# Hierarchical MoE block: top-two by the eight largest, gather and gate product by halves, one w_down load moved ahead of two up matrices

## What is computed

```python
    g_top_p, g_top = lax.top_k(g_prob, 1)
    e_in_group = jnp.take_along_axis(e_logits, g_top[:, :, None], axis=1)[:, 0]
    e_top_logit, e_top = lax.top_k(e_in_group, EXPERT_TOPK)
    gate = g_top_p * jax.nn.softmax(e_top_logit, axis=-1)
    ...
    h = (jax.nn.silu(jnp.einsum('td,edf->tef', xt, w_gate))
         * jnp.einsum('td,edf->tef', xt, w_up)
         * combine[..., None].astype(x.dtype))
    return jnp.einsum('tef,efd->td', h, w_down).reshape(nb_, s_, d_)
```

## Time and profile before

| what | value |
|---|---|
| median of 3 runs | 416.0 us (415.92 to 416.49) |
| the profiled execution | 415.13 us |
| its span, first to last instruction | 413.4 us |
| PE busy / weight loads / DVE / ACT / POOL | 90% / 73% / 40% / 33% / 8% of the span |
| DMA, mean over the span | 321 GB/s |
| mean granted TensorE clock | 0.963 of full speed |

### The profile page before, as it was taken

How to read it: one execution, slowest core, us unless ns; L and a number is a source line. 1 busy time by engine, 2 the same in 40 slices (tenths; PEclk the granted TensorE clock), 3 DMA queues, 4 the chain that set the end, 5 groups by cost and what they waited for, 6 DMA issues and landing times.

```text
span 413.4 us, 8388 instructions
## 1 busy us (share of the span) xinstructions
PE 373.6 (90%) x3461; PEld 302.3 (73%) x3461; DVE 166.4 (40%) x334; ACT 135.6 (33%) x235; POOL 33.3 (8%) x46
## 2 busy tenths in 40 slices
PE   7899899999999999999799999968797398499993
PEld 7899898889899999999767676744565156257653
DVE  2653667777264645554640212191202002012026
ACT  3553455734445444425523131301213013011010
POOL 7000000000000000001000002393000000000004
PEclk9999999999999999999999999998899599599998
DMA  8789884766568676699869999999999999999932
GB/s 275 204 316 371 278 291 153 269 219 205 188 203 298 184 253 186 212 412 426 364 230 423 419 420 422 419 419 418 423 420 420 422 419 421 420 421 419 380 104 101
DMA packets 51956, 132.78 MB, mean 321 GB/s; under 512 B 2978, under 2 KB 37810, under 8 KB 40660
## 3 DMA queue, kind: packets, MB, share of 16 engines
q1 hardware_dynamic: 51620, 132.14, 83.7%
q0 software_dynamic: 304, 0.17, 0.3%
HBM read 131.25 MB, written 1.05 MB: 320 GB/s over the span
## 4 chain that ended last, share of the span: by engine, by line
PE 66%; DMA 13%; DVE 9%; SPq 7%; ACT 3%; issue 2%; POOL 0%; DVEq 0%; ACTq 0%; POOLq 0%
PE bank L1073 25%; DMA gu<-in_w_up 13%; PE bank L1314 11%; PE bank L1192 5%; PE bank L1346 5%; SPq L375 5%; PE bank L1125 4%; PE bank L1269 4%; PE bank L1355 3%; PE bank L1169 3%; DVE wl L752 2%; PE bank L1081 2%; ACT wh L592 1%; SPq L380 1%; PE bank L1237 1%
## 5 line engine op out<-in xcount | busy, mean ns | idle before, releaser
L752 DVE TENSOR_TENSOR wl<-raw,wh 128x1024 fp32r<-128x1024 f32 x54 | 65.9, 1224 | 65.8 <-ACT wh L592 65.5
L1073 PE MATMUL bank<-xh,wh 128*128 128x256 f32 x288 | 82.8, 287 | 1.5 <-DVE wl L798 1.5
L1073 PE MATMUL bank<-xl,wh 128*128 128x256 f32 x288 | 81.5, 283 | 0.0
L1073 PE MATMUL bank<-xh,wl 128*128 128x256 f32 x288 | 81.4, 283 | 0.0
L1314 PE MATMUL bank<-gu,xg 128*32 128x256 f32 x1024 | 63.2, 408 | 19.6 <-DMA gu<-in_w_up 19.6
L592 ACT ACTIVATE wh<-raw 128x1024 fp32r<-128x1024 f32 x54 | 56.7, 1056 | 61.8 <-PE bank L1073 34.4
L1314 PEld LDWEIGHTS bank<-gu,xg 128*32 128x32 f32 x1024 | 34.4, 117 | 46.0 <-issue 27.1
L1073 PEld LDWEIGHTS bank<-xh,wh 128*128 128x128 f32 x288 | 55.2, 192 | 4.1 <-issue 2.0
L1073 PEld LDWEIGHTS bank<-xl,wh 128*128 128x128 f32 x288 | 55.2, 192 | 0.2 <-issue 0.2
L1073 PEld LDWEIGHTS bank<-xh,wl 128*128 128x128 f32 x288 | 55.2, 192 | 0.0
L1269 PE MATMUL bank<-pick,x1p 128*128 128x128 f32 x288 | 33.7, 275 | 1.3 <-DVE pick L957 1.3
(11 more groups left out here) (205 smaller groups left out, 469.6 us busy)
## 6 DMA issues: line engine op xcount, KB each, us to landing
gu<-in_w_up SPq DMA_DIRECT2D x32, 1024.0 KB, 23.4
gu<-in_w_gate SPq DMA_DIRECT2D x28, 1024.0 KB, 18.8
dn<-in_w_down SPq DMA_DIRECT2D x25, 1024.0 KB, 16.2
raw<-in_w_in SPq DMA_DIRECT2D x40, 512.0 KB, 4.7
raw<-in_w_o SPq DMA_DIRECT2D x8, 512.0 KB, 4.6
gu<-in_w_gate SPq DMA_DIRECT2D x8, 512.0 KB, 7.7
raw<-in_w_out_conv SPq DMA_DIRECT2D x4, 512.0 KB, 3.6
raw<-in_w_out_attn SPq DMA_DIRECT2D x4, 512.0 KB, 4.6
```

Source lines behind the costliest of these rows:

```text
L752: dve.tensor_tensor(wl[:, s, :].rearrange("p (k c) -> p k c", k=KC), raw[:, pair % NRAW, :].rearrange("p (k c) -> p k c", k=KC) [:, :, n % ...
L1073: mm = pe.matmul(dst, w[:, k, :], v[:, i, :], start=(i == 0 and w is h and v is high_in), stop=(i == len(ks) - 1 and w is l))
```

## The change

Five edits.
- The two `first_max` on 32 columns and the masking between them are replaced by `dve.max` (the eight largest of a row) and `dve.max_index` (their positions), once per tile each, and one compare of the first two positions with 0 to 31, which makes both hot rows.
- `slot_id` starts at FAR in place of 0, so `rank` keeps its offset and L952 goes. The counts (L951) are taken behind `pick_slots(0)`, waited for, and `rank_read` is signalled by an engine_nop.
- `gather(c, g)` makes half g. Half 0 stands where gather stood (the first needs only `pick_done` and `x1p_done`); half 1 is issued between k = 3 and k = 4 of the gate product. The wait for the picks is one per tile, at the first chunk.
- DVE's first `take_gathered` goes behind the gates' weights and `weigh_slots(1, 0)`.
- SP issues two of quad 2's four w_up matrices behind quad 1's last w_down. WARM_ROUTE goes from 14 to 9.

```diff
-WARM_ROUTE = 14
+WARM_ROUTE = 9
...
             sp.wait_ge(gu_ps, over)
-            load_gu(0, 2, parts=[1])
+            load_gu(0, 2, [0, 1], parts=[1])
             sp.wait_ge(y_ps, NY * over)
             for e in range(NE_EARLY, QE):
                 load_dn_one(1, e)
+            load_gu(0, 2, [2, 3], parts=[1])
             for e in range(NE_EARLY):
                 load_dn_one(2, e)
...
-            first_max(masked, expert_key[:, :], NE, top1, eq, hot1, tmp)
-            link(dve.scalar_tensor_tensor(masked, hot1, 100.0 * MASKED, masked, ALU.mult, ALU.add))
-            first_max(masked, expert_key[:, :], NE, top2, eq, hot2, tmp)
+            for t in range(TT):
+                ins = dve.max(top[:, t, :], masked[:, t, :])
+            link(ins)
+            for t in range(TT):
+                ins = dve.max_index(top_id[:, t, :], top[:, t, :], masked[:, t, :])
+            link(ins)
+            link(dve.tensor_tensor(hot[:, :, :, :], expert_id[:, :].unsqueeze(1).unsqueeze(1).to_broadcast(
+                [P, TT, 2, NE]), top_id[:, :, 0:2].unsqueeze(3).to_broadcast([P, TT, 2, NE]), ALU.is_equal))
...
-            dve.tensor_reduce(rf[:, 0, NQ:2 * NQ], counts, AX.X, ALU.max).then_inc(rank_read, 1)
-            link(dve.tensor_scalar(rank[:, :, :], rank[:, :, :], -FAR, None, ALU.add))
...
             pick_slots(0)
+            link(dve.tensor_reduce(rf[:, 0, NQ:2 * NQ], counts, AX.X, ALU.max))
+            dve.engine_nop().then_inc(rank_read, 1)
...
-            take_gathered(1)
...
             weigh_slots(1, 0)
+            take_gathered(1)
...
-            def gather(c):
-
-                pe.wait_ge(pick_done, 2 * c + 2)
-                for k in range(KC):
+            def gather(c, g):
+
+                for k in range(g * KHALF, (g + 1) * KHALF):
                     for t in range(TT):
-                        mm = pe.matmul(bank[4 + k // 4][:, (k % 4) * P:(k % 4 + 1) * P], x1p[:, t, k, :],
+                        if g == 0 and k == 0:
+                            pe.wait_ge(pick_done, 2 * c + t + 1)
+                        mm = pe.matmul(bank[4 + g][:, (k % 4) * P:(k % 4 + 1) * P], x1p[:, t, k, :],
                                        pick[:, t, :, :].rearrange("p e s -> p (e s)"),
                                        start=(t == 0), stop=(t == TT - 1))
-                    if k % 4 == 3:
-                        mm.then_inc(xg_ps, 1)
-
+                mm.then_inc(xg_ps, 1)
+
+            pe.wait_ge(x1p_done, TT)
+            gather(0, 0)
             pe.wait_ge(rank_read, 1)
-            pe.wait_ge(x1p_done, TT)
-            gather(0)
             pe.wait_ge(rounds_done, 1)
...
                             for k in range(KC):
+                                if part == 0 and k == KHALF:
+                                    gather(c, 1)
...
-                        gather(c + 1)
+                        gather(c + 1, 0)
```

More of the change, by code:

```diff
@@ L206, in hybrid_block @@
         rt_scope = ExitStack()
-        rt = sb("rt", [P, 13, TT, NL], where=rt_scope)
+        rt = sb("rt", [P, 7, TT, NL], where=rt_scope)
+        top = sb("top", [P, TT, 8], where=rt_scope)
+        top_id = sb("top_id", [P, TT, 8], mybir.dt.uint32, rt_scope)
+        hot = sb("hot", [P, TT, 2, NE], where=rt_scope)
         rt_scope.close()
@@ L226, in hybrid_block @@
         result = gu0[:, 0, 0, :, :].rearrange("p k c -> p (k c)").rearrange("p (t d) -> p t d", t=TT)
-        e_in, e_out = (rt[:, i, :, 0:NG + 1] for i in (11, 12))
+        e_in, e_out = (rt[:, i, :, 0:NG + 1] for i in (5, 6))
         x_in = [sem(f"x_in{t}") for t in range(TT)]
```

18 lines of the change are left out of this document (9 added, 9 removed).

## The result

The changed kernel takes **419.49 us** (median of 5 runs, 418.45 to 420.84); the kernel before, on the same chip in the same session, 415.92 (5 runs, 414.64 to 416.49). The ratio is 1.0082 with a 95% interval of 1.0051 to 1.0112: slower, by 3.6 us. Predicted were 420.4, range 415.4 to 422.6, and the way there was in the main the one forecast.

What follows compares the result with a forecast made beforehand. Bound by TensorE's rounds 0 to 2 until 260 us, the weight load stream until 357, then TensorE alone. Stream 1.1 us late plus 3.3 behind 357 gives +4.4 on 416.0: 420.4 us, range 415.4 to 422.6.

Steps and rivals of the forecast that it cites:

- step 5: Load stream at round 2's down product: the 2.1 us lead is lost, stream dry at 261.9, then 1.1 us late.
- Read-outs stay covered: Rival: TensorE never waits for gathered read-outs or loop bounds, first product 3.3 us earlier, total 414.5 us; chance 14%.
- the new operations do not do what they are for: Rival: `max` or `max_index` cost over three passes, routing no shorter, 1.1 us later everywhere, total 421.5; chance 6%.
- It cancels: Rival: quick semaphores and cheap top-two leave the stream 2 us ahead at 260, tail adds 2.6, total 416.5; chance 8%.
- The clock falls in round 0: Rival: new waits in round 0 drop TensorE's clock, 1.7 us more, total 422.1; chance 14%.
- Step 1: Routing's top-two on VectorE: `max`, `max_index` and one compare save 1.1 us (0.2 to 1.5).
- Step 2: Ranks to picks on VectorE: offset kept and counts taken behind save 0.3 us.
- Step 3: Round 0's first gate product, behind half a gather and the bound read: starts 2.1 us earlier.
- P: The time at which VectorE's picks end ahead of round 0, 202.97 us in the kernel before.
- Step 4: Every round: new TensorE waits of 0.83 us (ACT's read-out) and 0.72 (VectorE's); round 2's down product 3.6 later.
- Step 6: Behind the last weight wait at 357 us, rounds 6 and 7: half gathers and read-outs exposed, +3.3 us (2.8 to 3.6).

Runs made afterwards that it cites:

- halves_only: The kernel before with only the gather cut in halves, and VectorE's first read-out behind the weights; old routing and load order: 420.35 us.
- whole_gather: The changed kernel with the gather back in one piece at the end of a round, all else kept: 413.46 us.
- tail_whole: The changed kernel with whole gathers in the last two quads only (6 and 7): 415.60 us.
- route_alone: The kernel before with only the new top-two routing and 9 warming matmuls: 414.64 us.
- peeled_first: The changed kernel with round 0 written out ahead of TensorE's wait for the loop bounds, quad 0 fixed at one round: 418.04 us.
- stream_kept: The changed kernel with two of quad 4's w_gate loads issued ahead of the wait for round 2's down product: 418.41 us.
- orders_back: The changed kernel with the old order of quad 2's w_up loads and the old 14 warming matmuls: 419.71 us.
- halves_round0: peeled_first with the gather in halves in round 0 only, whole gathers from then on: 411.71 us.
- peeled_whole: peeled_first with whole gathers in every round: 415.23 us.

## Why the prediction was right, and by how much its terms were off

**Sign, place and mechanism.** The forecast case is the one that came: routing shorter, two holes a round, the stream dry once more at 262 to 272 us, a longer tail. halves_only and whole_gather show the two sides separately (+4.1 and -2.8 us on the kernel before), and tail_whole shows that of the 6.0 us between whole_gather and the changed kernel 3.9 are the tail. The two sides don't add up to +3.6: beside the halves the gain at the top is lost, as step 5 has it, since from the dip on the stream goes by round 2's down product. "Read-outs stay covered" fell with the two holes in round 1 and "the new operations do not do what they are for" with route_alone. "It cancels" had the routing right, which did save 1.6, and no lead was left to cancel with. "The clock falls in round 0" did not occur in the changed kernel's profile: round 0's products run at full speed (1.93 for the first 32 matmuls, as in round 1). It did occur in route_alone's, where it cost the gather 1.6 us for a price of 1.7.

**Step 1** (1.1, bounds 0.2 to 1.5): 1.60, just outside. I priced `max` and `max_index` by whole passes of the earlier trace rows; with the link behind them the MAX8 pair took 0.32 where I took 0.45, and the four index instructions, overlapping, 0.46 where I took 0.86. The number of instructions that the Trainium skill names (Vector Engine (DVE) Microarchitecture Reference, section 3.9: a value load and a find behind the max pass) is what the trace shows; what failed is my price of each.

**Step 2** (0.3): 0.26 us from the ranks to the picks, as taken. The picks end 1.9 earlier, for 1.4.

**Step 3** (first product 2.1 earlier, at P + 3.2): it came at P + 3.85 with P = 202.08, against P + 3.88 before. The bound read, which I took at 0.8 between 0 and 1.5, takes its upper bound: 1.50 from the CAST's end to the first matmul. The right size was in the earlier trace rows (VectorE's 1.50, for two reads and the loop entry), and halving it was the mistake. With the read out of the way (peeled_first) the product starts at P + 2.6, for the 2.7 of my lower end. The errors of steps 1 and 3, 0.5 too little and 0.65 too much, cancel by luck: first release 1.96 earlier, for 2.1.

**Step 4** (0.83 + 0.72 a round): the profile shows holes of 0.55 and 0.51, but it also lets a half gather last 1.95 and 2.05 where I reckoned with a slot of 1.84. What doesn't depend on that is the time from a half gather's start to the product behind it: 2.50 for ACT's (224.95 to 227.45), where I had 2.67, and 2.56 for VectorE's (229.31 to 231.87), where I had 2.55. From the gather's start to the transposes round 1 takes 12.24 us where it took 10.71 (223.19 to 233.90, the row below, of before): 1.53 more, for 1.55.

```profile
233.90 0.44 PE L1324 MATMUL bank<-ident,pickw 128*128 128x128 f32 x2
```

By the w_down issues round 1 grew by 1.2 us only, since its down product lost a small gap of before, and round 2 by 1.5. Round 2's w_down: +3.5, for +3.6.

**Step 5** (2.1 lead lost, quad 6 1.1 late): the products are 1.75 late in the profiled pair, and the stream 1.4 late by the bytes moved. The step said that the stream keeps its 2.1 us until round 2 and loses them there. That part failed: only 0.6 us were left by then, since the restart ran at 286 GB/s where the kernel before had 354 with the same loads. The forecast didn't suffer, because it went by the bytes behind round 2's down product, which came as late as forecast whatever lead there was. What suffered is the expectation of stream_kept, which counted on that lead: about 1 us was to be had, not 3.6.

**Step 6** (+3.3, 2.8 to 3.6): +2.83 against the one profile of before, +3.27 against tail_whole piece by piece, and 3.9 by the medians of tail_whole and after. Its last piece, forecast at 1.84 + 0.72 = 2.56, measured 2.68. The mechanism (half a gather and a read-out behind the DMA wait, twice) stands as told.

**Costed at nothing and so measured:** the order of loads and the warming (orders_back). The moved `take_gathered` and the extra waits of rounds 3 and 4 were not tried alone, so no run shows what they cost.

**The sum.** +4.4 predicted, +3.6 by the medians of one session, +3.5 on the 416.0 given: 0.8 to 0.9 too high. The profiled pair has +4.6.

**Open:** why the same half loads restart the stream at 285 to 301 GB/s in some kernels and at 340 to 354 in others, and with it how much of halves_round0's gain is the early release and how much the faster restart; whether peeled_whole and whole_gather differ.

## What to carry to other kernels

Cutting a producer in two so that its consumer can start early is worth it only where the consumer was waiting for it, which here was one round in eight; in every other round the whole gather was the cover for two read-outs on other engines, and the cut put both on the path. Look for what an operation hides before moving it, and apply the cut by stage: halves in the first round alone gave 411.7, halves everywhere 419.5. And an earlier release of a load is worth the bytes that it has moved when the next wait comes, not its microseconds: of a 2 us lead 1.4 were gone after a slow restart of the stream, and the wait for round 2 would have taken the rest.

## What the runs showed of the hardware that was not expected

- **TensorE's clock can fall while TensorE is busy.** In four profiled executions (halves_only, stream_kept, peeled_first, orders_back) the warming matmuls behind the narrow logits product (128x36) ran at half clock, and the ranks came 0.6 to 2.2 us late. The warming of the changed kernel, then of peeled_first, then of orders_back, with the window of it and VectorE's rank that waited (the other profiled executions have no such stretch):

```profile
198.45 2.17 PE L1133 MATMUL bank<-ident 128*128 128x128 f32 x18
```

```profile
198.30 3.31 PE L1133 MATMUL bank<-ident 128*128 128x128 f32 x18
```

```profile
198.17 4.55 PE L1132 MATMUL bank<-ident 128*128 128x128 f32 x28
```

```profile
198.00:200.00 2.00, 2.00 (x10) 1.91 (x10) 1.79 (x13) 1.98 (x2) 0.00 (x0) 0.50 1.01 414
```

```profile
202.87 0.22 DVE L956 SCALAR_TENSOR_TENSOR rank<-bank,chosen 128x64 f32<-128x64 f32 x1 [2.43 <-PE bank L1267]
```

  A granted clock of 0.50 is the 1.2 GHz level; PE was busy for the whole 2 us. With 28 warming matmuls the 4.55 us outlast the shorter routing, and the rank waits 2.43 for TensorE. The medians of orders_back and of the changed kernel are alike all the same (419.71, 419.49), and in which executions the clock falls the runs don't tell.
- **How fast an empty queue restarts differs.** These are single profiled executions, and whether it goes by the kernel or by the execution the runs don't tell. The same eight 512 KB loads (4 KB packets) moved 286 GB/s in 9 us in the changed kernel, 354 before and 343 in halves_round0, each with the DMA engines 0.89 to 1.00 busy; 1 MB loads (8 KB packets) moved 409. A 4 KB packet took 218 ns in the changed kernel from 209 to 215 us and 159 ns from 219 on, once w_up loads were queued behind; at 159 ns the same small packets move 404 to 426 GB/s.
- **VectorE is held up beside GpSimd's work on SBUF.** In the kernel before, round 3's `pickw` (6.84 us) and `pick` (3.79) ran beside POOL's work on `x1n` (265.37 to 279.17). In the changed one, where that work ends at 279.59, only `pickw` meets it (before, then changed):

```profile
268.57 6.84 DVE L1003 TENSOR_TENSOR pickw<-pick,comb 128x128 f32<-128x128 f32 x2
275.73 3.79 DVE L957 TENSOR_TENSOR pick<-slot_id,rank 128x128 f32<-128x128 f32 x2 [0.24 <-DVE rank L1006]
```

```profile
275.74 4.19 DVE L1010 TENSOR_TENSOR pickw<-pick,comb 128x128 f32<-128x128 f32 x2
280.25 0.49 DVE L964 TENSOR_TENSOR pick<-slot_id,rank 128x128 f32<-128x128 f32 x2 [0.24 <-DVE rank L1013]
```

  `pick` takes 0.49 there, and the round, by its w_down issues, 21.8 us in place of 26.6. It didn't reach the total, since TensorE then waited longer for weights (7.05 us before round 4's products at 298.81). The Trainium skill (SBUF — State Buffer, "Who interferes with whom") tells of a port pair that the two engines share and lock; these durations agree.
- **A load's landing lags far behind its issue when the queue is deep:** quad 2's last w_down took 18.9 us (whole_gather) and 19.2 (peeled_whole), long enough for a product that was ready 16 us behind the issue to wait for it.
